# Row sums of adaLN joined with the router in pieces, an early first half of an expert, and the mixers' products spread out

## The chip, the core and the metric

The program runs on one core of one Trainium2 chip. The metric is the time of one execution in device microseconds (us). Times of single instructions come from one profiled execution; the median of the runs is given beside it. TensorE has a matmul side (PE) and a weight-load side (PEld); VectorE is DVE, ScalarE is ACT, GpSimd is POOL and SyncE, which issues most DMAs, is SP. PSUM has eight banks of 128 x 512 floats.

## The reference

Two blocks in a row on 256 tokens of width 1024. Only the parts around the change are shown.

```python
def first_block(x, ...):
    ...
    x = x + merged @ w_o[l]
    h2 = rmsnorm(x, g_ffn[l]).reshape(B * S, D)
    moe = hier_moe(h2, w_rg[l], b_rg[l], w_re[l], b_re[l], w_up[l], w_down[l])
    return x + moe.reshape(B, S, D)

def hier_moe(h, ...):            # 4 groups of 8 experts
    g_logits = h @ w_rg + b_rg   # top-1 group
    e_logits = h @ w_re + b_re   # top-2 experts inside the group
    ...                          # weights of the chosen experts: combine
    for n in range(N_EXPERTS):
        a, b = jnp.split(h @ w_up[n], 2, axis=-1)
        out = out + combine[:, n:n + 1] * ((jax.nn.silu(a) * b) @ w_down[n])

def second_block(x, c, ...):     # two layers
    mod = c_act @ w_ada[l] + b_ada[l]           # nine vectors of adaLN
    h = h + 0.5 * (1.0 + gt1) * swiglu(hn, ...)
    proj = hn @ w_mix_in[l]
    # window attention | RWKV-7 recurrence | short convolution (3 taps)
    mixed = jnp.concatenate([y_att, y_rwkv, y_conv], axis=-1) @ w_mix_out[l]
    h = h + (1.0 + gt2) * mixed
    h = h + 0.5 * (1.0 + gt3) * swiglu(hn, ...)
```

The recurrence of RWKV-7 subtracts `S kk` and adds `v k` to a state S at each token. In the kernel it is worked out in chunks of 64 tokens, so that a triangular matrix of each chunk has to be inverted.

## The kernel before

**Products and banks.** Every engine runs its own instruction list, written out by hand in `build`; the order in it is the order of the work, and semaphores join the engines. On PE, `product(consumer)` hands out banks 0 to 6 in a ring of seven: the n-th product waits until the (n-7)-th has been read by ACT or DVE. `keep_warm(n)` multiplies a matrix of ones with a constant n times, 256 columns each; nobody reads the result. An f32 matmul stands in the trace as two rows, one of type fp32r as one row.

**Start.** PE transposes x (`to_features`), sums squares (`norm_sum`), turns the rows of gains into columns (`to_columns(5)`), and then projects with slabs of `w_in`, 1 MB each, which SP streams into six slots.

**Router and experts.** After the projection `w_o`, DVE norms h in eight chunks and makes the low part `h_lo` of each at once (`norm(..., split=True)`). PE waits for all eight, does the router's 16 matmuls (36 columns each), turns h into tokens (`to_tokens`, into `htok`, f32), and DVE finds each token's group. DVE then signals `ids_ready`, on which SP starts to load experts in the order of the groups; it builds the gathering matrices `perm` and the weights `cin`. `moe` gathers the tokens of the other three groups in eight chunks of 384 columns, `htok` times `perm` in f32, from banks 2 to 7; ACT writes the high part `hg_hi`, DVE the low part. Then come the experts: group 0 in full (eight units of two steps s of 128 tokens), the others in 24 units of one step ("few"). An up matmul is three fp32r ones of 512 columns (high x high, high x low, low x high); `up_high` on ACT and `up_low` on DVE split each slab, `w_hi` has three places. Meanwhile DVE does the row sums of adaLN (`ada_piece`, 1.2 us each).

**Mixers, one in each layer.** After a projection split in parts comes the RWKV chain. `short` are six blocks of eight matmuls for the short convolution's inputs. Four coupling products (AT, BT, C1T, C2T) of eight 64-row matmuls each are masked on DVE. Six levels double the size of the inverted blocks: `off*Tm` on PE, a copy on ACT, `TT*M1` and `M1*TT` on PE, subtractions on DVE; each level also takes a step of window attention, and levels 0 to 3 one `short` block. Then four chunks update the state, the convolution is done on DVE, y is centred and normed, and the output projection runs: four of its eight blocks begin early with the six inputs that are ready (`OUT_EARLY`), `residual` on DVE adds the blocks to x. Before that, DVE splits three slabs of the next dense part (`up_low`); the third one can be loaded only when the first slab of `w_mix_out` is released.

## Time and profile before

| | us |
|---|---|
| median of 3 runs | 1969.59 |
| lowest, highest | 1968.55, 1969.59 |
| the profiled execution | 1968.42 |
| its span, first to last instruction | 1966.6 |
| PE, PEld busy | 1898.4, 1696.2 |
| DVE, ACT busy | 1135.5, 756.5 |

1.8 us of the profiled execution lie outside its span. A row of a timeline gives the start and the length in us, the engine, the line, the output and inputs, and how many instructions are merged; in square brackets, the idle time before it and who ended it. The granted clock (PEclk) of a stretch is a share of 2.4 GHz, so 0.50 is 1.2 GHz. A matmul that writes constants only (`bank<-const`) is a `keep_warm`.

### The profile page before, as it was taken

Reading aid. Unit: us, or ns where it says so; the run is one execution under the profiler, and the core shown is the slowest. Engines: PE = TensorE matmul, PEld = TensorE weight load, DVE = VectorE, ACT = ScalarE, POOL = GpSimd, SP = SyncE. Lnnn points to the kernel's source line nnn. Section 1 sums busy time; section 2 is a strip of 40 time slices with the busy share of each in tenths; the row PEclk is TensorE's granted clock in tenths of the full one; section 3 lists DMA queues with packets and bytes.
Section 4 is the critical chain, followed back from the end, with each engine's and each line's share of the span. In section 5 each row is a group of like instructions: output and inputs, shape, how many; then the busy total and the mean of one; then the engine's idle time right before and its main releaser. Section 6 shows DMA issues by size and latency. Waiting matters only on the chain.

```text
span 1966.6 us, 29769 instructions
## 1 busy us (share of the span) xinstructions
PE 1898.4 (97%) x12380; PEld 1696.2 (86%) x12380; DVE 1135.5 (58%) x1754; ACT 756.5 (38%) x1071; POOL 31.1 (2%) x63
## 2 busy tenths in 40 slices
PE   7999989999999999999999999999999999999998
PEld 6788868778876666999988879999999988879998
DVE  1394043366666655877646548776877547545543
ACT  3222231243444445434443324444444443324442
POOL 6000000000000000000000000000000000000000
PEclk9999999899999999999999999999999999999999
DMA  8244421256699988677541036787676541033441
GB/s 258 92 149 146 145 70 43 108 223 236 253 376 393 366 323 340 243 307 307 193 151 44 22 159 223 307 318 289 240 306 264 165 150 44 23 123 128 180 191 65
DMA packets 124566, 391.56 MB, mean 199 GB/s; under 512 B 11802, under 2 KB 72516, under 8 KB 95120
## 3 DMA queue, kind: packets, MB, share of 16 engines
q1 hardware_dynamic: 122192, 387.71, 52.8%
q8 instruction: 98, 1.61, 0.3%
q0 software_dynamic: 1936, 0.89, 0.2%
q10 hardware_dynamic: 304, 1.06, 0.1%
q14 instruction: 36, 0.29, 0.0%
HBM read 388.58 MB, written 1.05 MB: 198 GB/s over the span
## 4 chain that ended last, share of the span: by engine, by line
PE 87%; DVE 6%; issue 2%; ACT 2%; DMA 2%; SPq 0%; DVEq 0%; ACTq 0%
PE bank L534 86%; DMA slab<-in_w_up 2%; PE bank L569 1%; ACT w_hi L1403 1%; DVE slab_low L1837 0%; DVE hT L1799 0%; DVE tiny L1882 0%; DVE region L2382 0%; ACT L1290 0%; DVE hT L1822 0%; DVE region L1881 0%; ACT rsB L1326 0%; DVE region L2364 0%; DVE region L1901 0%; ACT region L1312 0%
## 5 line engine op out<-in xcount | busy, mean ns | idle before, releaser
L1837 DVE TENSOR_TENSOR slab_low<-slab,w_hi 128x2048 fp32r<-128x2048 f32 x152 | 348.0, 2291 | 216.2 <-ACT w_hi L1403 215.8
L534 PE MATMUL bank<-h_hi,w_hi 128*128 128x256 f32 x1408 | 395.3, 281 | 1.5 <-DVE h_lo L1829 1.5
L534 PE MATMUL bank<-h_lo,w_hi 128*128 128x256 f32 x1408 | 394.7, 280 | 0.0
L534 PE MATMUL bank<-h_hi,slab_low 128*128 128x256 f32 x1408 | 393.3, 279 | 0.0
L1403 ACT ACTIVATE w_hi<-slab 128x2048 fp32r<-128x2048 f32 x152 | 290.7, 1915 | 168.8 <-DMA slab<-in_w_ffn_in 81.9
L534 PEld LDWEIGHTS bank<-h_hi,w_hi 128*128 128x128 f32 x1408 | 264.3, 188 | 3.0 <-issue 3.0
L534 PEld LDWEIGHTS bank<-h_hi,slab_low 128*128 128x128 f32 x1408 | 265.8, 189 | 0.0
L534 PEld LDWEIGHTS bank<-h_lo,w_hi 128*128 128x128 f32 x1408 | 264.9, 188 | 0.0
L534 PE MATMUL bank<-gT_hi,d_hi 128*128 128x256 f32 x832 | 233.7, 281 | 0.8 <-DVE gT_lo L2024 0.8
L534 PE MATMUL bank<-gT_hi,d_low 128*128 128x256 f32 x832 | 233.6, 281 | 0.0
L534 PE MATMUL bank<-gT_lo,d_hi 128*128 128x256 f32 x832 | 233.6, 281 | 0.0
L534 PE MATMUL bank<-hT,slab 128*128 128x256 f32 x960 | 214.2, 383 | 2.1 <-DVE hT L1799 1.8
L534 PEld LDWEIGHTS bank<-hT,slab 128*128 128x128 f32 x960 | 183.2, 192 | 28.9 <-issue 4.1
L1437 ACT ACTIVATE lnt<-bank 128x256 f32<-128x256 f32 x128 | 48.9, 382 | 361.9 <-PE bank L534 359.7
L534 PE MATMUL bank<-region 128*128 128x128 f32 (+4 forms) x1296 | 168.6, 291 | 13.0 <-DVEq L2406 5.0
L534 PEld LDWEIGHTS bank<-region 128*128 128x128 f32 (+2 forms) x1296 | 148.8, 185 | 29.2 <-DVEq L2406 6.4
L534 PEld LDWEIGHTS bank<-gT_hi,d_hi 128*128 128x128 f32 x832 | 156.7, 188 | 1.3 <-issue 1.0
L534 PEld LDWEIGHTS bank<-gT_lo,d_hi 128*128 128x128 f32 x832 | 156.7, 188 | 0.3
L534 PEld LDWEIGHTS bank<-gT_hi,d_low 128*128 128x128 f32 x832 | 156.7, 188 | 0.0
L534 PE MATMUL bank<-region,slab 128*128 128x256 f32 x640 | 141.8, 380 | 1.6 <-DVEq L2177 1.1
L1312 ACT ACTIVATE region<-bank 128x256 f32<-128x256 f32 (+1 forms) x121 | 53.3, 452 | 221.9 <-PE bank L534 221.5
L534 PEld LDWEIGHTS bank<-region,slab 128*128 128x128 f32 x640 | 120.7, 190 | 20.7 <-issue 2.3
(295 smaller groups left out, 2640.6 us busy)
## 6 DMA issues: line engine op xcount, KB each, us to landing
slab<-in_w_ffn_in SPq DMA_DIRECT2D x88, 1024.0 KB, 8.5
slab<-in_w_up SPq DMA_DIRECT2D x64, 1024.0 KB, 9.2
region<-in_w_ada SPq DMA_DIRECT2D x112, 512.0 KB, 6.6
region<-in_w_ffn_out SPq DMA_DIRECT2D x44, 1024.0 KB, 5.0
region<-in_w_down SPq DMA_DIRECT2D x32, 1024.0 KB, 5.6
slab<-in_w_in SPq DMA_DIRECT2D x23, 1024.0 KB, 5.1
slab<-in_w_mix_in SPq DMA_DIRECT2D x20, 1024.0 KB, 8.9
hT<-in_w_ada SPq DMA_DIRECT2D x32, 512.0 KB, 6.0
```

Of the source, the lines that this page charges most:

```text
L534: return nc.tensor.matmul(o, lhsT, rhs, start=start, stop=True, skip_group_check=True)
L569: return nc.tensor.transpose(o, in_, C("eye")[0:k, 0:k])
L1312: read(nc.scalar.activation(dst, src, func, **kw))
L1403: nc.scalar.activation(w_hi[h % 3][:, :], slab[slot][:, :], ACT.Copy).then_inc(S["uhi_ready"], 1)
L1437: nc.scalar.activation(act_s, place(s)[:, 0:T], ACT.Silu).then_inc(S["silu_ready"], 1)
L1837: V_.tensor_tensor(slab_low[slot][:, :], slab[slot][:, :], w_hi[h % 3][:, :].bitcast(F), ALU.subtract)\
```

## The change

- `keep_warm` uses the first 256 columns of the constants (identity and ones), which arrive before the others, instead of `cos`. It is added at the start (4 before x, 3 before the sum of squares, 4 before the columns of gains), and 6 before the index logits; 10 before the router become 4.
- `norm` before the router no longer makes `h_lo`; `router_low` does so in three pieces between DVE's router steps. The router's matmuls run over the chunks of h outside and over tokens inside, with a matmul of constants of 128 columns between chunks.
- The tokens are gathered from two fp32r parts, `htok_hi` and `htok_lo`, each turned from `h_hi` and `h_lo`, with `perm` in fp32r. High and low land in two banks, so there are three places; ACT and DVE each copy one.
- `moe` on PE begins with the first half (four chunks, both steps) of expert 0, before the gather; the second half follows it. ACT and DVE split slabs 0 and 1 before `moe`, ACT with its copies of `htok_lo` and `permT` around them.
- Mixers: level 0 is formed directly (`TT` = identity minus the level-0 part of AT; `Tm` is its transpose). Only AT is coupled first; BT, C1T, C2T follow in levels 1 to 3. `short` blocks move: 0 before the low-rank products, 1 as before, 2 before the levels, 3 in level 1, 4 and 5 in halves of 128 tokens at the start of the four chunks. The convolution is done per 128 channels, the first after chunk 2. The sums of y go to bank 7, with the first early output blocks around them. Five places lose a `keep_warm` (4, 2, 2, 5, 3), one gains 3.

The core of the diff:

```diff
             def moe():
-                quiet()
                 members = [u for u in UNITS if u.seg == 0]
+                slabs_of(members[0])
+                keep_warm(5)
+                for s in range(2):
+                    ring_free(s)
+                for kc in range(KD // 2):
+                    for s in range(2):
+                        m = up_mm(members[0], s, s, kc)
+                m.then_inc(S["half_mid"], 1)
                 pe.wait_ge(S["tok_ready"], w("tok_ready"))
                 for kc in range(KD):
                     gather(kc)
-                pe.wait_ge(S["h_split"], w("h_split", KD))
-                for unit, t, s, pending in SLOTS_OF[0][:-1]:
+                quiet()
+                for s in range(2):
+                    for kc in range(KD // 2, KD):
+                        m = up_mm(members[0], s, s, kc)
+                    m.then_inc(S["up_done"], 1)
+                turn_step(0)
+                for unit, t, s, pending in SLOTS_OF[0][2:-1]:
...
             norm_sum()
-            keep_warm(10)
-
-            for i in range(KD):
+            keep_warm(4)
+
+            idle, ps = product(None), product("dve")
+            for kc in range(KD):
                 pe.wait_ge(S["hn"], w("hn"))
-            ps = product("dve")
-            for t in range(NT):
-                for kc in range(KD):
+                for t in range(NT):
                     m = mm(ps[:, t * 64:t * 64 + 36], hT[:, kc, t * P:(t + 1) * P], router[:, kc, :],
                            t == 0 and kc == 0)
+                if kc < KD - 1:
+                    mm(idle[:, 0:P], C("ones"), const[:, 0:P], True)
             m.then_inc(S["for_dve"], 1)
...
-                    keep_warm(4)
+                    short = projection(hT, 4, "act")
+                    short(0)
                     pe.wait_ge(S["lora_in"], w("lora_in"))
...
-                    for lev in range(6):
+                    short(SHORT_FIRST)
+                    for g in range(2):
+                        pe.wait_ge(S["tt_ready"], w("tt_ready"))
+                        ps = product("act")
+                        for x in range(4):
+                            m = transpose(ps[:, x * P:(x + 1) * P], V["TT"][:, g, x * P:(x + 1) * P])
+                        m.then_inc(S["for_act"], 1)
+                    pe.wait_ge(S["kdup_ready"], w("kdup_ready"))
+                    scores(0)
+                    for lev in range(1, 6):
...
-                        if lev:
-                            output(lev - 1)
-                        if SHORT_FIRST + lev < 6:
-                            short(SHORT_FIRST + lev)
+                        if lev in COUPLED:
+                            coupling(*COUPLED[lev][1:3])
+                        output(lev - 1)
+                        if lev == 1:
+                            short(SHORT_FIRST + 1)
...
                     for c4 in range(T // CHUNK):
                         t, r0 = c4 // 2, (c4 % 2) * CHUNK
+                        short_half(4 + c4 // 2, c4 % 2)
...
-                        keep_warm(2)
+                        if c4 > 1:
+                            keep_warm(2)
...
-                    keep_warm(5)
+                    pe.wait_ge(S["swa_ready"], w("swa_ready"))
+                    pe.wait_ge(S["conv_ready"], w("conv_ready"))
...
+                    out_early(0)
                     pe.wait_ge(S["y_ready"], w("y_ready"))
-                    pair_sum(V["W"], consumer="dve")
-                    keep_warm(3)
+                    mm(bank[7][:, :], C("half"), V["W"], True).then_inc(S["y_mean"], 1)
+                    out_early(1)
                     pe.wait_ge(S["yc_sq"], w("yc_sq"))
                     pair_sum(sq[:, 0:2, :])
...
+                    for b in range(2, OUT_EARLY):
+                        out_early(b)
```

**Where the order moves, PE, router to first expert.** `rscratch,const` is the count of groups, `const,hT` and `const,h_hi` the turning into tokens, `region,sq` the gather. Before:

```order
L534 MATMUL bank<-const 128x256 x10
L534 MATMUL bank<-router,hT 128x36 x16
L569 MATMUL bank<-const,hT 128x128 x8
L534 MATMUL bank<-rscratch,const 128x4 x5
L569 MATMUL bank<-const,hT 128x128 x8
L534 MATMUL bank<-const 128x256 x6
L569 MATMUL bank<-const,region 128x128 x6
L534 MATMUL bank<-const 128x256 x2
L534 MATMUL bank<-rscratch,region 128x8 x6
L534 MATMUL bank<-region,sq 128x384 x16
L534 MATMUL bank<-w_hi_59,h_hi 128x512
```

And after, from the router's last pair:

```order
L538 MATMUL bank<-router,hT 128x36 x2
L579 MATMUL bank<-const,h_hi 128x128 x8
L538 MATMUL bank<-rscratch,const 128x4 x5
L579 MATMUL bank<-const,h_hi 128x128 x8
L538 MATMUL bank<-const 128x256 x4
L579 MATMUL bank<-const,h_lo 128x128 x16
L579 MATMUL bank<-const,perm_r 128x128 x6
L538 MATMUL bank<-const 128x256 x4
L538 MATMUL bank<-rscratch,perm_r 128x8 x6
L538 MATMUL bank<-const 128x256 x5
L538 MATMUL bank<-w_hi_59,h_hi 128x512
```

Sixteen transposes are new, and 24 matmuls of expert 0 now stand where 16 of the gather stood; the gather's 32 come behind them.

**PE, a mixer's coupling and first levels.** `region 128x128` are couplings and levels, `const,region` turned probabilities, `hT,slab` a `short` block. Before:

```order
L534 MATMUL bank<-region,const 128x512
L569 MATMUL bank<-const,region 128x128 x12
L534 MATMUL bank<-region 128x128 x32
L534 MATMUL bank<-region,const 128x256 x2
L534 MATMUL bank<-region 128x128 x26
L534 MATMUL bank<-hT,slab 128x256 x8
L534 MATMUL bank<-region 128x128 x10
L569 MATMUL bank<-const,region 128x128 x2
L534 MATMUL bank<-region 128x128 x16
L534 MATMUL bank<-region 64x128 x2
L534 MATMUL bank<-hT,slab 128x256 x8
```

And after, to the end of level 1:

```order
L538 MATMUL bank<-region,const 128x512
L538 MATMUL bank<-region 128x128 x8
L579 MATMUL bank<-const,region 128x128 x12
L538 MATMUL bank<-region,const 128x256 x2
L538 MATMUL bank<-hT,slab 128x256 x8
L579 MATMUL bank<-const,region 128x128 x8
L538 MATMUL bank<-region 128x128 x12
L579 MATMUL bank<-const,region 128x128 x2
L538 MATMUL bank<-region 128x128 x24
L538 MATMUL bank<-region 64x128 x2
L538 MATMUL bank<-hT,slab 128x256 x8
```

24 of the 32 coupling matmuls left the front for levels 1 to 3, and eight transposes stand where level 0's 24 matmuls stood.

**PE, the end of a mixer.** `region,slab` is the output projection, `region,const 128x512` the sums of y, `sq,const` those of its squares. Before:

```order
L534 MATMUL bank<-region 64x128 x8
L534 MATMUL bank<-const 128x256 x5
L534 MATMUL bank<-region,const 128x512
L534 MATMUL bank<-const 128x256 x3
L534 MATMUL bank<-sq,const 128x512
L534 MATMUL bank<-region,slab 128x256 x64
```

And after:

```order
L538 MATMUL bank<-region 64x128 x8
L538 MATMUL bank<-region,slab 128x256 x6
L538 MATMUL bank<-region,const 128x512
L538 MATMUL bank<-region,slab 128x256 x6
L538 MATMUL bank<-sq,const 128x512
L538 MATMUL bank<-region,slab 128x256 x52
```

Twelve matmuls of the projection took the place of the constants. The squares' product, which takes a bank of the ring, now stands behind the second block of the projection instead of before the first; the sums of y left the ring.

## Rows read from the trace of the kernel before

**Rows 1.** The page: busy time of each engine; the chain, shares by engine.
```profile
PE 1898.4 (97%) x12380; PEld 1696.2 (86%) x12380; DVE 1135.5 (58%) x1754; ACT 756.5 (38%) x1071; POOL 31.1 (2%) x63
...
PE 87%; DVE 6%; issue 2%; ACT 2%; DMA 2%; SPq 0%; DVEq 0%; ACTq 0%
```

**Rows 2.** Timeline, start: start us, length us, engine, line, instructions merged.
```profile
11.79 5.76 PE L534 MATMUL bank<-sq,const 128*128 128x256 f32 x16 [1.60 <-ACT sq L1331]
...
18.91 3.26 DVE L1799 SCALAR_TENSOR_TENSOR hT<-xT,par,rsB 128x256 f32<-128x256 f32 x8
```

**Rows 3.** Timeline from the norm before the router to the gather.
```profile
361.08 1.67 DVE L1799 SCALAR_TENSOR_TENSOR hT<-xT,par,rsB 128x256 f32<-128x256 f32 x4 [3.99 <-ACT rsB L1326]
...
365.94 5.57 PE L534 MATMUL bank<-router,hT 128*128 128x36 f32 x32 [1.53 <-DVE hT L1799]
...
371.62 0.23 DVE L2204 TENSOR_TENSOR rscratch<-bank,bbc 128x72 f32<-128x72 f32 x1 [4.46 <-PE bank L534]
...
375.81 0.16 DVE L2225 COPY tiny<-bank 128x4 f32<-128x4 f32 x1 [1.93 <-PE bank L534]
...
379.62 2.14 SPq L2488 DMA_DIRECT2D slab<-in_w_up  x4
...
386.08 10.56 PE L534 MATMUL bank<-region,sq 128*128 128x384 f32 x32 [0.40 <-issue]
```

**Rows 4.** Windows: length, busy (count) of five engines, PEclk, DMA share, GB/s.
```profile
368.00:370.00 2.00, 2.00 (x11) 2.00 (x11) 0.00 (x0) 0.00 (x0) 0.00 (x0) 0.50 0.00 0
...
402.00:404.00 2.00, 2.00 (x6) 1.52 (x6) 1.51 (x1) 0.00 (x0) 0.00 (x0) 0.50 0.99 410
```

**Rows 5.** The page's costliest groups: splitting a slab, on DVE and on ACT.
```profile
L1837 DVE TENSOR_TENSOR slab_low<-slab,w_hi 128x2048 fp32r<-128x2048 f32 x152 | 348.0, 2291 | 216.2 <-ACT w_hi L1403 215.8
...
L1403 ACT ACTIVATE w_hi<-slab 128x2048 fp32r<-128x2048 f32 x152 | 290.7, 1915 | 168.8 <-DMA slab<-in_w_ffn_in 81.9
```

**Rows 6.** Timeline: the start of step s = 3 (expert 1, second step) on PE.
```profile
419.82 0.51 PE L534 MATMUL bank<-w_hi,h_hi 128*128 128x512 f32 x1 [1.51 <-DVE gT_lo L1970]
```

**Rows 7.** The chain of waits: 24 up matmuls of 512 columns, in the steady run.
```profile
434.52 5.50 PE bank L534 x24
```

**Rows 8.** Timeline, mixer of the first layer: couplings, levels, first chunk.
```profile
1040.21 5.04 PE L534 MATMUL bank<-region 64*128 64x128 f32 x64
...
1041.47 0.69 DVE L2364 TENSOR_TENSOR region<-bank,const 128x512 f32<-128x512 f32 x1 [1.01 <-PE bank L534]
...
1057.23 2.59 PE L534 MATMUL bank<-region 128*128 128x128 f32 x20
...
1078.42 2.59 PE L534 MATMUL bank<-region 128*128 128x128 f32 x20
...
1081.04 0.42 DVE L1881 SCALAR_TENSOR_TENSOR region<-bank,const 128x256 f32<-128x256 f32 x1 [3.36 <-PE bank L534]
...
1089.01 3.00 PE L534 MATMUL bank<-region 128*128 128x128 f32 x20
...
1105.01 2.66 PE L534 MATMUL bank<-region 128*128 128x64 f32 x16 [0.49 <-DVEq L2389]
```

**Rows 9.** Timeline: the starts of the second and third chunk on PE.
```profile
1113.74 3.77 PE L534 MATMUL bank<-region 128*128 128x64 f32 x16 [1.22 <-DVEq L2406]
...
1125.69 1.60 PE L534 MATMUL bank<-region 128*128 128x64 f32 x12
```

**Rows 10.** Windows, columns as in rows 4: two microseconds of the second chunk.
```profile
1116.00:1118.00 2.00, 2.00 (x7) 1.24 (x6) 0.46 (x1) 0.00 (x0) 0.00 (x0) 0.50 0.00 0
```

**Rows 11.** Timeline, end of the mixer: output projection, third slab, residual.
```profile
1145.77 27.79 PE L534 MATMUL bank<-region,slab 128*128 128x256 f32 x128
...
1164.66 1.91 ACT L1403 ACTIVATE w_hi<-slab 128x2048 fp32r<-128x2048 f32 x1 [10.87 <-DMA slab<-in_w_ffn_in]
...
1168.82 4.27 DVE L2185 SCALAR_TENSOR_TENSOR xT<-bank,modg,xT 128x256 f32<-128x256 f32 x7
```

More of the change, by code:

```diff
@@ L124 @@
     "ulo_ready": "the low part of half of a unit's up weights", "dlo_ready": "that of its down weights",
-    "gt_lo": "a step's turned activations, low part", "hg_split": "both parts of a chunk of the gathered h",
+    "gt_lo": "a step's turned activations, low part", "hg_low": "a chunk of the gathered h, low part",
     "h_split": "both parts of a chunk of the normalised residual",
@@ L1070, in _ @@
             m.then_inc(S["for_dve"], 1)
-            to_tokens(1)
-            keep_warm(6)
+            to_tokens(h_hi, 1)
+            keep_warm(4)
+            pe.wait_ge(S["h_split"], w("h_split", KD))
+            for t in range(NT):
+                to_tokens(h_lo, t)
             pe.wait_ge(S["perm_ready"], w("perm_ready"))
@@ L1125, in _ @@
                     pair_sum(sq[:, 6, :])
-                    short = projection(hT, 6, "act")
-                    for b in range(SHORT_FIRST):
+                    for b in range(1, SHORT_FIRST):
                         short(b)
@@ L1677, in _ @@
                 tables(SIG)
+                short = [V[dst][:, c, :] for dst in ("cb", "cc", "ch") for c in range(2)]
                 act.wait_ge(S["pm_ready"], w("pm_ready"))
@@ L1815, in norm, with router_low @@
                                          ALU.subtract).then_inc(S["h_split"], 1)
+            def router_low(first, end):
+                for j in range(first, end):
+                    dve.wait_ge(S["h_high"], w("h_high"))
+                    V_.tensor_tensor(h_lo[:, j, :], hT[:, j, :], h_hi[:, j, :].bitcast(F), ALU.subtract)\
+                        .then_inc(S["h_split"], 1)
             def norm_dense(gain, shift):
@@ L2196, in _ @@
             link(V_.memset(clist, PAD))
+            norm(xT, lambda j: col("g_ffn", j), hT)
+            router_low(0, 1)
             def wide(v, n):
```

203 lines of the change are left out of this document (121 added, 82 removed).

## The prediction

> **What bounds the kernel now.** The page's first part and its chain come first: PE is busy 97% of the span and holds 87% of the chain [rows 1]. So only what shortens or slows PE's list counts, and it can shorten in three ways: matmuls that nobody reads go, a wait goes, or the same matmul runs at 2.4 instead of 1.2 GHz. Next come the timeline of PE at the places of the change, for its waits, and the windows there, for the clock. Both PEclk windows near the router and the one in a chunk show 0.50 [rows 4, 10].
>
> Prices for one matmul: 5.50/24 = 0.229 us for 512 columns [rows 7], so 0.172 for 384; 27.79/128 = 0.217 for a row of 256 f32 columns [rows 11], so a `keep_warm` matmul (two rows) costs 0.43 and a `short` block (16 rows) 3.47; a coupling product is 5.04/4 = 1.26 [rows 8]. The sum is made against the profiled execution, 1968.42.
>
> **Start: -1.2.** The first `norm_sum` takes 5.76 for 16 rows [rows 2] where 16 x 0.217 = 3.47 is the quick price: 2.3 to gain if constants before it bring the quick pace. The four constants before `to_columns` cost about 1.0 (partly beside ACT's squares). DVE's norm, which starts at 18.91 [rows 2], then starts at about 17.7. Bounds: -2.5 (those four are covered) and +1.0 (the pace doesn't come). I take the middle, since the matmuls just ahead are what differs from the quick places. The six before the index logits (2.6) I put at nothing: they stand where PE waits for DVE anyway; uncovered they cost 2.6.
>
> **Router to experts: -3.1.**
> - DVE's four last norm steps start at 361.08 with a step of 1.67/4 = 0.42, and the router's 5.57 begin at 365.94, after all eight [rows 3]. In pieces, the first matmuls start with the first chunk; 32 rows of 0.118 (36 columns, clock now full) and seven constants of 128 columns (14 rows, 0.115) are 5.4 us. With the first chunks at about 361.8 PE ends at 367.2 and DVE adds the bias at 367.4 instead of 371.62: -4.2. The count of groups likewise, 375.81 to 371.7: -4.1, as `router_low(1, 6)` (some 2.0) lies beside the transposing of `h_hi`. Uncovered it would add up to 2.
> - SP's first w_up moves from 379.62 [rows 3] to about 375.5. 1.5 MB (weights and slab 0) at 410 GB/s [rows 4] are 3.8, with 1.2 of latency (estimate): slab 0 is there at 380.5. ACT then does `up_high(0)` (1.92 [rows 5]) to 382.4, four copies of `htok_lo` (512 columns; estimate 2.1) to 384.5, `up_high(1)` to 386.4, and only then `permT`, to 387.0. The second step's bank is the one that this copy frees, so PE starts its first up matmul at about 387.1, after an idle stretch near 381.
> - Then 24 ups 5.5 [rows 7], to 392.6; gather 32 x 0.172 = 5.5 instead of 10.56 [rows 3], to 398.1; second half 5.5, to 403.6. Then the steps of turning, each behind `hidden` or DVE's `up_low` (2.29 [rows 5]) and a piece of adaLN: about 1.1, 2.7 and 2.0 of idle, and the rest of the first unit. Step s=3 starts at 415.6 instead of 419.82 [rows 6]: -4.2.
> - The idle stretch before expert 0 may drop the clock, as it stands at 0.50 at 402:404 [rows 4] behind today's wait for slab_low: +1.1. Net -3.1. Behind it the experts keep the shift, since PE or the loads set their pace as before. Bounds: -8 (no wait before the first half) and 0 (all given back to the waits for slabs).
>
> **Mixers: -10.8 each, -21.6 in all.** Stamps are of the first layer's mixer [rows 8].
> - The chain up to the couplings stays (the moved `short(0)` takes 3.47 where four constants took 1.7; the second gain, a warmer clock, gives it back). DVE's first AT mask stands at 1041.47, after 1.01 of idle; with AT alone in front it stands at 1040.5.
> - Of DVE's masks of four couplings and the subtractions of level 0, eight steps of about 0.69 remain before level 1, with small gaps: 5.8, so its inputs are ready at 1046.3 and PE starts level 1 at 1046.4 instead of 1057.23: -10.8. What PE drops is 24 coupling matmuls (3 x 1.26, moved) and level 0's products.
> - Level 1 has to wait for its probabilities: DVE's scaled comes 2.6 after a level's start (1081.04 - 1078.42), then ACT's exponentials; estimate +1.9. It also holds a coupling (1.26) and `short(3)` (3.47). Level 2 starts at 1060.5, 14.1 later.
> - Levels 2 and 3 lose the `short` (3.47) and gain a coupling (1.26). Today a level is (1078.42 - 1057.23)/2 = 10.6, 1089.01 - 1078.42 = 10.6; PE's list alone is then 10.6 - 3.47 + 1.26 = 8.4, and DVE's chain (scaled at +2.6, two subtractions with their products 4.4, the couple's two masks 1.4, probabilities 0.9, less overlap) gives 8.8. I take 8.8: level 3 at 1069.3, level 4 at 1078.2, against 1089.01.
> - Levels 4 and 5 had no `short`: 1105.01 - 1089.01 = 16.0 stays, chunk 0 at 1094.2: -10.8.
> - Chunks: two `short` blocks (in four halves of 1.74, 7.0) come in. Against that go the idle stretches (0.49 and 1.22 [rows 8, 9], and more inside a chunk), two `keep_warm(2)` (1.7), and the half clock of chunk 1 (0.50 at 1116:1118 [rows 10]; chunk 1 takes 1125.69 - 1113.74 = 11.95 [rows 9], full pace would save some 2 to 3). Net +1.0.
> - The end: the constants (5 + 3, 3.4) become output matmuls, and the convolution leaves a third of its time behind the last chunk. The projection's first matmul comes at about 1140.0 instead of 1145.77 [rows 11] on the old stamps, its early blocks end 4.0 sooner. But of its blocks p0 to p7, p6 now takes the bank of p0, since the squares' product sits between p1 and p2; before, p6 took the bank of that product, read long ago. p0 is read by DVE's residual, which starts at 1168.82 only, behind `up_low` of the third slab, for which ACT waits 10.87 on its DMA and starts at 1164.66 [rows 11]. That load is released by the projection, so it comes 4.0 sooner: ACT 1160.7, DVE's residual at 1164.9, first bank free at 1165.4. PE is at p6 at 1162.4: 3.0 of stall. So only 1.0 of the 4.0 stays.
> - Sum: -10.8 + 1.0 - 1.0 = -10.8. Bounds -17 (no stall, chunk 1 wins 3 more) and -4 (DVE sets levels 1 to 3, stall full).
>
> **Sum.** -1.2 - 3.1 - 21.6 = -25.9: 1942.5 for the profiled execution. The median of the runs lies 1969.59 - 1968.42 = 1.17 above it: 1943.7, I say 1943.5.
>
> **The rivals.**
> - *The third slab comes early enough.* Were it loaded before p6's turn, the 3.0 of stall fall away in both mixers: -6, 1937.5. For it: SP has fewer waits ahead once the blocks start earlier. Against: ACT's 10.87 of idle there is all DMA [rows 11]. 0.12.
> - *DVE becomes the engine of the levels.* A level's DVE work grows by two masks (1.4); if they lie on the loop from scaled to scaled, a cycle is 10 + 1.4 = 11.4 instead of 8.8: +2.6 for levels 2 and 3 and two mixers, +10, 1953.5. For it: DVE and PE already alternate there (3.36 of idle before scaled [rows 8]). Against: the same 3.36 is room enough for 1.4. 0.20.
> - *Transposes lower the clock.* Behind the 16 of `h_lo` the first half of expert 0 would run at 1.2 GHz like the row at 402:404 [rows 4]: 5.5 becomes up to 11, less what it waits for slabs anyway, some +2; level 0 gives +1 in each mixer. +4, 1947.5. The transposes by themselves are 24 of thousands. 0.07. The Trainium skill, "TensorE: Matmul & The Clock Gate", § Part 4: PE-mode transpose, speaks for it: a matmul in transpose mode doesn't bring the full clock on, since it isn't counted as a busy PE in the same way. By that rule the sum would be -22, by the row alone -26; no run so far shows which.
> - *Slower: the levels lose their cover.* Levels 2 and 3 lose the solid 16 rows of `short`, and levels hang on DVE between small products. If the granted clock falls to 0.50 in levels 2 to 5, each one of PE's 6 us of matmuls doubles: +6 in each of 4 levels and two mixers, +48: 1991. It decides from the fifth of the eight levels on (5 x 6 = 30 > 25.9). Against: levels 4 and 5 of today have no `short` and still run their first 20 rows in 3.00 [rows 8], 0.150 a row beside 2.59/20 = 0.130 in level 3. 0.05.
> - *The change doesn't do what it says*: fewer constants leave the router at 0.50 as today [rows 4] (+2), inside the forecast's range.
>
> **Chances.** 0.56 for the forecast, whose own bounds from the parts are about 1936 to 1951; then as above. The range 1932 to 1954 takes in the early slab and DVE's levels. A measurement can tell about 0.2%, 4 us, from no change, here 1965.7 to 1973.5. Faster 0.92 (all but the last rival, and a small remainder where several losses meet), same 0.03, slower 0.05.
>
> **What would show it.** In the profile after: DVE's bias add some 4 us earlier; PEclk 1.00 while the router runs; the first up matmul waits on ACT's copy, at about 387, and s=3 starts near 415.6 (all less the start's 1.2); level starts of PE 14, 8.8 and 8.8 apart, with PE, not DVE, idle for the shorter time; the chunks one by one within 1 us of before; a gap of 3 us in front of the seventh block of the output projection, ended by DVE's residual, with ACT waiting for the third slab's DMA. It would be wrong if levels 2 and 3 take over 10, if PEclk shows 0.50 in a level, or if the steps after expert 0's second half wait for slabs more than 6 us in all.

## The result and the profile of the changed kernel

The changed kernel takes 1944.7 us (median of 4 runs, 1941.4 to 1949.9), the kernel before, beside it, 1969.1. The ratio is 0.9885 with a 95% interval of 0.9861 to 0.9909: faster. The profiled execution took 1947.8, its span is 1946.0. So the forecast of 1943.5 came out for the median. For the profiled execution it was 1942.5, and that one is 5.3 longer. The stages of the two profiles tell how much of this was right.

Both kernels do `norm_sum` (`bank<-sq,const`, 16 rows) before each large part, and its start divides the span. Stages in us, before and after, as the difference of two such starts:

| stage | before | after | moved | forecast |
|---|---|---|---|---|
| start, to 36.93 | 36.93 | 35.95 | -1.0 | -1.2 |
| attention and projections, to 356.48 | 319.55 | 316.47 | -3.1 | 0 |
| router and experts, to 776.15 | 419.67 | 419.69 | 0.0 | -3.1 |
| first dense part, to 969.68 | 193.53 | 193.53 | 0.0 | 0 |
| first mixer, to 1173.40 | 203.72 | 194.99 | -8.7 | -10.8 |
| two dense parts and second mixer, to 1763.73 | 590.33 | 581.02 | -9.3 | -10.8 |
| the last dense part and the end | 202.87 | 204.35 | +1.5 | 0 |

The page of the changed kernel, the engines and the chain, to be held against [rows 1]: PE has 17.3 us less to do and is as much the bound as before.

```profile
PE 1881.1 (97%) x12374; PEld 1684.9 (87%) x12374; DVE 1131.8 (58%) x1746; ACT 759.9 (39%) x1079; POOL 31.1 (2%) x63
...
PE 86%; DVE 6%; ACT 3%; issue 2%; DMA 2%; SPq 0%; DVEq 0%; ACTq 0%
```

The timeline of the start (start us, length us, then as in [rows 2]). `norm_sum` takes 3.72 instead of 5.76, and DVE's norm starts at 17.93 instead of 18.91, 0.2 from the forecast of 17.7. Between them stand 1.89 us of constants, which nothing covers.

```profile
11.77 3.72 PE L538 MATMUL bank<-sq,const 128*128 128x256 f32 x16 [0.83 <-ACT sq L1400]
15.33 1.89 PE L538 MATMUL bank<-const 128*128 128x256 f32 x8
...
17.93 3.26 DVE L1873 SCALAR_TENSOR_TENSOR hT<-xT,par,rsB 128x256 f32<-128x256 f32 x8
```

The timeline from the router to the experts, in order of time, against [rows 3, 6]. Everything here stands 4.06 earlier already before the router (352.42 against 356.48).

```profile
363.08 0.23 DVE L2282 TENSOR_TENSOR rscratch<-bank,bbc 128x72 f32<-128x72 f32 x1 [2.13 <-PE bank L538]
...
377.51 1.91 ACT L1472 ACTIVATE w_hi<-slab 128x2048 fp32r<-128x2048 f32 x1 [2.98 <-DMA slab<-in_w_up]
379.33 2.04 ACT L1381 ACTIVATE htok_lo<-bank 128x512 fp32r<-128x512 f32 x4
...
380.05 1.83 PE L538 MATMUL bank<-rscratch,perm_r 128*128 128x8 f32 x12 [4.46 <-ACT htok_lo L1381]
381.73 4.62 PE L538 MATMUL bank<-const 128*128 128x256 f32 x10
...
383.30 0.85 ACT L1381 ACTIVATE region<-bank 128x512 f32<-128x512 f32 x2
...
385.78 0.99 PE L538 MATMUL bank<-w_hi,h_hi 128*128 128x512 f32 x1
...
414.94 0.47 PE L538 MATMUL bank<-w_hi,h_hi 128*128 128x512 f32 x1 [1.64 <-DVE gT_lo L2051]
```

And a window there (length, busy and count of five engines, PEclk, DMA share, GB/s):

```profile
384.00:386.00 2.00, 2.00 (x7) 1.64 (x5) 1.79 (x1) 1.43 (x2) 0.00 (x0) 0.50 0.97 410
```

DVE's bias add is 8.5 earlier than 371.62, so 4.5 of its own. By s=3 only 4.88 - 4.06 = 0.8 are left. In between PE waits 4.46 for ACT's copies of `htok_lo`, and the five constants behind that wait run at 1.2 GHz: 4.62 instead of 2.2. ACT's copies of `permT`, on which the first up matmul was thought to wait, are done at 384.15 (383.30 + 0.85), but PE comes to it only at 385.78.

The timeline of the first mixer, against [rows 8, 9]. `bank<-hT,slab` is a short block, DVE's rows are the start of `scaled` in levels 2 and 3 and that of the next one, the `128x128` block is the half at the start of chunk 0.

```profile
1042.63 3.33 PE L538 MATMUL bank<-region 64*128 64x128 f32 x24
...
1057.11 2.59 PE L538 MATMUL bank<-region 128*128 128x128 f32 x20
...
1059.73 0.42 DVE L1962 SCALAR_TENSOR_TENSOR region<-bank,const 128x256 f32<-128x256 f32 x1 [3.62 <-PE bank L538]
...
1068.57 0.42 DVE L1962 SCALAR_TENSOR_TENSOR region<-bank,const 128x256 f32<-128x256 f32 x1
...
1077.84 0.69 DVE L1962 SCALAR_TENSOR_TENSOR region<-bank,const 128x512 f32<-128x512 f32 x1 [0.60 <-PE bank L538]
...
1090.24 2.05 PE L538 MATMUL bank<-hT,slab 128*128 128x128 f32 x16
...
1124.89 4.52 PE L538 MATMUL bank<-region,slab 128*128 128x256 f32 x12 [1.36 <-issue]
```

Level 1 starts near 1042.7, level 2 at 1057.1 (14.4 later), then `scaled` follows itself by 8.84 and 9.27. Chunk 0 begins at 1090.24. With the 4.04 by which the mixer starts earlier, 1105.01 becomes 1100.97, so the front of the mixer gave 10.7: forecast 10.8.

The end of both mixers, against [rows 11]: PE's early and late blocks, ACT's split of the third slab, DVE's residual, and PE's resumption, in the first layer and in the second.

```profile
1133.55 15.70 PE L538 MATMUL bank<-region,slab 128*128 128x256 f32 x72
...
1147.18 1.91 ACT L1472 ACTIVATE w_hi<-slab 128x2048 fp32r<-128x2048 f32 x1 [5.61 <-DMA slab<-in_w_ffn_in]
...
1151.33 3.63 DVE L2264 SCALAR_TENSOR_TENSOR xT<-bank,modg,xT 128x256 f32<-128x256 f32 x6
...
1151.96 8.83 PE L538 MATMUL bank<-region,slab 128*128 128x256 f32 x32 [2.71 <-DVE xT L2264]
...
1733.27 8.54 PE L538 MATMUL bank<-region,slab 128*128 128x256 f32 x32 [2.78 <-DVE xT L2264]
```

That is the stall that was forecast, with the engine that was named: 2.71 and 2.78 of it, 3.0 said. But the 32 rows behind it (p6 and p7) take 8.83 and 8.54, where 32 x 0.217 is 6.9, and the first early blocks take 4.52 for 12 rows, where 2.6 is the quick price. The windows say why:

```profile
1126.00:1128.00 2.00, 2.00 (x6) 1.56 (x5) 0.00 (x0) 0.00 (x0) 0.00 (x0) 0.50 0.00 0
...
1152.00:1154.00 2.00, 2.00 (x6) 1.64 (x7) 1.56 (x4) 0.83 (x2) 0.00 (x0) 0.61 1.03 424
```

### The profile page after: what moved, and what is told of

Same layout as the page of the kernel before. It is cut to its first block, busy times and chain, and to the rows that moved or that the text cites. A ratio compares the mean times of both kernels' runs of the same rounds, so it can differ in the third digit from the quotient of the medians.

```text
span 1946.0 us, 29754 instructions
## 1 busy us (share of the span) xinstructions
PE 1881.1 (97%) x12374; PEld 1684.9 (87%) x12374; DVE 1131.8 (58%) x1746; ACT 759.9 (39%) x1079; POOL 31.1 (2%) x63
## 3 DMA queue, kind: packets, MB, share of 16 engines
HBM read 388.58 MB, written 1.05 MB: 200 GB/s over the span
## 4 chain that ended last, share of the span: by engine, by line
PE 86%; DVE 6%; ACT 3%; issue 2%; DMA 2%; SPq 0%; DVEq 0%; ACTq 0%
PE bank L538 85%; DMA slab<-in_w_up 2%; PE bank L579 1%; ACT w_hi L1472 1%; DVE slab_low L1918 1%; DMA slab<-in_w_ffn_in 0%; DVE region L1931 0%; ACT rsB L1395 0%; DVE region L1982 0%; DVE tiny L1963 0%; DVE region L2470 0%; DVE region L2447 0%; DVE region L2468 0%; DVE hT L1903 0%; DVE region L1962 0%
## 5 line engine op out<-in xcount | busy, mean ns | idle before, releaser
L538 PE MATMUL bank<-hT,slab 128*128 128x256 f32 (+1 forms) x1024 | 215.2, 370 | 1.7 <-DVE hT L1873 1.2
L538 PE MATMUL bank<-region 128*128 128x128 f32 (+5 forms) x1200 | 154.7, 288 | 6.7 <-DVEq L2435 2.4
L538 PE MATMUL bank<-region,slab 128*128 128x256 f32 x640 | 147.9, 390 | 9.8 <-DVE xT L2264 5.5
L538 PEld LDWEIGHTS bank<-region 128*128 128x128 f32 (+2 forms) x1200 | 135.0, 181 | 22.1 <-issue 4.6
L2008 DVE SCALAR_TENSOR_TENSOR region<-region 128x1024 f32<-128x1024 f32 x112 | 136.4, 1220 | 1.6 <-DMA region<-in_w_ada 1.6
```

What stands on the lines that cost most here:

```text
L538: return nc.tensor.matmul(o, lhsT, rhs, start=start, stop=True, skip_group_check=True)
L2008: V_.scalar_tensor_tensor(part, part, 1.0, c_act, ALU.mult, ALU.mult, accum_out=ada[:, o:o + 1])\
```

## The experiments

**The theory** going in: the gain is the front of the mixers, and each mixer gives some of it back in a stall of the ring, whose price is more than its idle time. **The rival**: the gain comes as well from the new router and from a clock that happened to be full at 50 and 290 us. First the two halves of the change by themselves. The median of the kernel before, timed beside the first four variants, was 1964.9 (17 runs, 1959.1 to 1978.7).

**The mixers alone.** The kernel before with, for the mixers only, everything that the change does:

```diff
-                    for lev in range(6):
+                    for lev in range(1, 6):
...
+                        if lev in COUPLED:
+                            coupling(*COUPLED[lev][1:3])
...
+                        short_half(4 + c4 // 2, c4 % 2)
...
+                    out_early(0)
```

> The kernel before with the mixers' part of the change alone (level 0 formed directly, the couplings and short blocks spread, the new end). In the profile of the changed kernel each mixer moved by 8.7 and 9.3 us (from the squares' sum before it to the one behind it, 1026 and 1173 before). If the parts add, this kernel gains 18 us: about 1951, and its other stages stay within 2 us of before. Rival: part of what the mixers gain is only a clock that was full by chance in one profile; then this kernel shows half clock at other places in the mixers and gains 12 or less. The end stall before the seventh output block (2.7 us, ended by DVE's residual) should be there in both mixers.

Measured: 1945.7 us, 19.3 below the kernel before (18 expected), ratio 0.9885 (0.9859 to 0.9911), as the whole change had. In the profile the first mixer is 10.1 shorter than before, the part to 1740.70 behind it 10.5: forecast 10.8 each. The stall is there in both (first and second layer), somewhat longer. But in the second the clock is 1.00 behind it (1734:1736), and the same 32 rows take 7.14 instead of 8.83:

```profile
1152.23 8.83 PE L536 MATMUL bank<-region,slab 128*128 128x256 f32 x32 [3.04 <-DVE xT L2220]
...
1733.72 7.14 PE L536 MATMUL bank<-region,slab 128*128 128x256 f32 x32 [3.01 <-DVE xT L2220]
```

The rest of the profile is not as before everywhere, though: the experts' stage took 417.5 instead of 419.7 with unchanged code. About 2 us of one profile's stage there are not the change's.

**The start, the router and the experts alone.**

```diff
+            keep_warm(4)
             to_features(xin, "x_in")
+            keep_warm(3)
             norm_sum()
+            keep_warm(4)
...
+            up_high(0)
             for t in range(NT):
                 for x in range(2):
-                    evac(htok[:, t, x * 512:(x + 1) * 512], 512)
+                    evac(htok_lo[:, t, x * 512:(x + 1) * 512], 512)
```

> The kernel before with the start, the router and the experts' part alone, the mixers as before. Theory: start -1.0 (adaLN's first slabs arrive on time either way), router to step s=3 of the experts -0.8 only, since the first half of expert 0 waits for constants at half clock and runs half its matmuls at half clock; the rest, about 3 us between 46 and 292 us, was the clock of stretches that the change doesn't touch. Then this kernel gains 2 to 5 us: about 1965. Rival: the stretches at 46:52 and 288:292 run at full clock because of the new start; then they are at full clock here too and it gains 5 to 7, about 1963.

Measured: 1961.8 us, ratio 0.9992 (0.9965 to 1.0019): by time, no difference that these runs can tell, 3.1 us between the medians. In the profile the start gave 1.05; the stage to the router took 319.57, as before, with PEclk 0.50 at 50:52 and 0.64 at 290:292. So the new start alone doesn't always bring the full clock there. Whether it makes it likelier stays open: of the eleven profiles of this case that have the constants in front of the first sum, or transposes in their place, eight show the full clock near 290 and three, this one among them, the half; the three without either (the kernel before, the mixers alone, and the start without constants) show the half. From the router's `norm_sum` to the third turning of activations (`bank<-const,lnt`, in step s=3) it was 66.2 before, 63.1 here: -3.1, the term of the sum. The changed kernel's own profile shows 65.3 for the same code: its clock stayed at 0.50 up to near 388. Over all eight profiles that have this code here unchanged (the changed kernel, this one and six below) it is 62.1 to 65.7, so that -3.1 is one draw between -0.6 and -4.1. The rival is half right: 3 us of the changed profile's 20.6 are the clock of a stretch that the change doesn't touch, but they don't carry the gain.

**The squares' bank, taken earlier.**

```diff
+                    sq_bank = product("act")
                     out_early(0)
...
-                    pair_sum(sq[:, 0:2, :])
+                    mm(sq_bank[:, :], C("half"), sq[:, 0:2, :], True).then_inc(S["for_act"], 1)
```

> The changed kernel, with one edit at the end of a mixer: the bank for the squares' product is taken before the first early output block instead of between the second and the third, so that the seventh block (p6) takes a bank that was read long ago. Theory of the prediction (the stall is the price of the ring's order): the wait of 2.7 us before p6 goes, and the half clock behind it (1152 to 1156) with it; p7 then waits for the bank of p0, up to 1 us: -2 to -4 per mixer, 4 to 8 in all, about 1939. Rival: the wait only moves to p7 and to the next dense part, whose first units need DVE's low parts and norm anyway: -1 or less in all.

Measured: 1934.1 us, ratio 0.9829 (0.9803 to 0.9855), faster than both kernels, and by more than I expected. The projection runs in one piece:

```profile
1126.86 22.61 PE L538 MATMUL bank<-region,slab 128*128 128x256 f32 x104
...
1140.58 1.91 ACT L1473 ACTIVATE w_hi<-slab 128x2048 fp32r<-128x2048 f32 x1 [5.69 <-DMA slab<-in_w_ffn_in]
...
1144.73 4.26 DVE L2265 SCALAR_TENSOR_TENSOR xT<-bank,modg,xT 128x256 f32<-128x256 f32 x7
```

The third slab and DVE's residual come as late, relative to PE, as with the stall (14.6 and 18.7 behind the squares' sum, 14.5 and 18.6 with it). Only the bank is another. From the squares' sum to the next `norm_sum` it is 1149.31 - 1126.01 = 23.3; in the changed kernel 27.9 and 27.7, with the mixers alone 28.3 and, in the second layer, 26.6. The stall's whole price is thus 4.4 to 5.0 where the clock falls behind it, and 3.2 in the one mixer where it doesn't: 2.7 to 3.0 of idle time, and a clock at 0.50 that costs most of the rest. The remaining part of the 6.3 that the first mixer gained over the changed kernel is the other half-clock stretch (1126:1128), absent here although PE's rows and waits before it are the same (0.66 and 1.36 of idle). It isn't the bank's doing alone: two later profiles with the bank edit have it in their first mixer (4.24 and 4.48 for these 12 rows instead of 2.83), while the second mixer of the changed kernel and both with the mixers alone lack it. Why it falls in some and not in others stays open.

Nor does the edit rule the stall out. In one of the 18 mixers profiled with it, the first of the start without constants below, the third slab is split 17.3 behind the squares' sum instead of 14.6, and PE waits in front of the last block:

```profile
1145.72 1.91 ACT L1471 ACTIVATE w_hi<-slab 128x2048 fp32r<-128x2048 f32 x1 [8.38 <-DMA slab<-in_w_ffn_in]
...
1150.40 5.41 PE L538 MATMUL bank<-region,slab 128*128 128x256 f32 x16 [1.93 <-DVE xT L2263]
```

**Filling the wait before the experts.**

```diff
-            keep_warm(4)
+            keep_warm(14)
             pe.wait_ge(S["cin_ready"], w("cin_ready"))
```

> The changed kernel with 14 instead of 4 constants matmuls before the product of the weights (L1116's keep_warm(4)), which fill the 4.46 us in which PE waits for ACT's copy of htok_lo. Theory: the half clock at 381 to 387 comes from that idle stretch; with it filled the granted clock stays at 1.00, the five constants behind take 2.2 instead of 4.6, and the first half of expert 0 starts 1.6 earlier and ends 2.5 earlier; step s=3 starts 1 to 2.5 earlier. Rival: ACT and DVE with the next slabs set the first units, so step s=3 stays within 0.5 us of 414.9 and only the clock figures change.

Measured: 1941.1 us, ratio 0.9859 (0.983 to 0.9887).

```profile
371.75 6.21 PE L538 MATMUL bank<-const 128*128 128x256 f32 x28
...
381.74 0.47 PE L538 MATMUL bank<-w_hi,h_hi 128*128 128x512 f32 x1 [0.19 <-ACT region L1381]
```

The clock stays at 1.00 (382:384), and the first up matmul now does wait on the copy of `permT`, as the prediction had said for the changed kernel. From the router's sum to the third turning it is 62.2, against 65.3 in the changed kernel's profile and 63.5 in that of the bank edit. These pairs give 1.3 to 3.1. But the code without the filling took 62.1 in its shortest profile, so that the gain lies in not losing the clock near 381, and isn't shown beyond that. The two mixers stall as in the changed kernel: 28.0 and 28.1 from the squares' sum to the next `norm_sum`. By time the intervals of the two kernels overlap (0.9830 to 0.9887, 0.9861 to 0.9909).

**Both edits.**

```diff
-            keep_warm(4)
+            keep_warm(14)
             pe.wait_ge(S["cin_ready"], w("cin_ready"))
...
+                    sq_bank = product("act")
                     out_early(0)
```

> The changed kernel with both edits: the squares' bank taken before the early output blocks, and 14 constants before the product of the weights. If the two gains add (11 and some 3 us against the changed kernel's own median) it stands 3 us below the kernel with the bank edit alone, about 1931, with one half-clock stretch fewer near 381. Rival: the half clock only moves to another place (the wait near 404), then it is within 1 us of the kernel with the bank edit alone.

Measured: 1928.0 us (1927.4 to 1930.7), ratio 0.981 (0.9788 to 0.9832); the kernel before, beside this and the next three variants, had 1965.4. This is the best version that was timed more than once, 1.9% below the kernel before where the change alone was 1.15%. That it beats the bank edit alone (0.9803 to 0.9855) is likely, not shown: the intervals overlap. The third turning comes 62.6 behind the router's sum, the mixers are as with the bank edit alone (188.7 for the first). While PE works, the profile has PEclk below 0.97 in two stretches only, near 366 and near 407.

**All couplings in front again.**

```diff
                     coupling("be", "al")
+                    for lev in COUPLED:
+                        coupling(*COUPLED[lev][1:3])
...
-                        if lev in COUPLED:
-                            coupling(*COUPLED[lev][1:3])
```

and the same for `couple` on DVE.

> The kernel with the bank edit, but all four coupling products and their masks in front of the levels again, as in the kernel before; the rest of the change stays. Theory: in levels 1 to 3 DVE is busy without a gap (cycle 8.84 us, of which the two masks are 1.45), so spreading the masks only moves them. Here level 1 starts 6 x 0.72 = 4.3 us later and levels 1 to 3 are 1.4 shorter each: +0 to +1.5 per mixer, the level cycle 7.4. Rival (that of the change's design): masks are free inside the levels; then the cycle stays above 8.5 and each mixer is 4 us longer.

Measured: 1947.9 us, ratio 0.9903 (0.9876 to 0.993). This expectation was wrong: the mixers are 9.2 and 6.5 longer than with the bank edit alone, not 0 to 1.5. DVE's six masks, PE's products of level 1, and the turnings of levels 2 and 3:

```profile
1041.99 4.32 DVE L2448 TENSOR_TENSOR region<-bank,const 128x512 f32<-128x512 f32 x6
```

```profile
1050.60 3.33 PE L538 MATMUL bank<-region 64*128 64x128 f32 x24
...
1067.65 0.44 PE L579 MATMUL bank<-const,region 128*128 128x128 f32 x2
...
1075.81 0.44 PE L579 MATMUL bank<-const,region 128*128 128x128 f32 x2
```

The levels shrink by less than the two masks: 8.16 between turnings instead of 8.90, since PE now waits 0.74 for DVE in between. And the front grows by more than the masks: level 1 starts 28.46 behind the sum of squares (1050.60 - 1022.14), with the masks spread 19.57 (1037.64 - 1018.07). Of these 8.9 the masks are 4.3; PE also waits 1.98 and 2.01 for banks that DVE's masks free, its clock is at 0.50 from 1038 to 1046, and `short(2)` comes behind all that. So the spread was worth 6.5 to 9.2 in a mixer, half-clock stretches of both mixers' fronts included. Forming level 0 directly, the other half of the front's gain, was not tried by itself.

**Short blocks 4 and 5 whole, in levels 2 and 3.**

```diff
-                        if lev == 1:
-                            short(SHORT_FIRST + 1)
+                        if lev < 4:
+                            short(SHORT_FIRST + lev)
...
-                        short_half(4 + c4 // 2, c4 % 2)
```

> The kernel with the bank edit, but short blocks 4 and 5 whole in levels 2 and 3 as before, not in halves in the chunks. Theory: levels 2 and 3 grow from 8.8 to about 12 (PE's list 8.6 + 3.47), the four chunks lose four halves of 1.9 but get idle stretches back, so they shrink by 5.5 at full clock: +1 per mixer; and if the clock falls in the chunks as in the kernel before (0.50 at 1114 to 1120), +4. Rival: the levels take the blocks for nothing beside DVE's chain; then each mixer is 5 us shorter.

Measured: 1957.6 us, ratio 0.9949 (0.9929 to 0.9969), each mixer 10.7 longer than with the bank edit. Levels 2 and 3 grew by 3.35 and 3.45, as expected. The four chunks, from chunk 0 to the first output matmul, did not shrink at all: 38.0 without the halves, 34.65 with them.

```profile
1097.46 2.66 PE L538 MATMUL bank<-region 128*128 128x64 f32 x16 [0.49 <-DVEq L2474]
...
1105.39 3.21 PE L538 MATMUL bank<-region 128*128 128x64 f32 x16 [1.22 <-DVEq L2504]
...
1135.47 2.83 PE L538 MATMUL bank<-region,slab 128*128 128x256 f32 x12 [1.36 <-issue]
```

```profile
1110.00:1112.00 2.00, 2.00 (x10) 1.91 (x9) 0.68 (x5) 1.37 (x6) 0.00 (x0) 0.50 0.03 8
```

The idle times of [rows 8, 9], 0.49 and 1.22, are back, and the clock is at 0.50 from 1108 to 1124. The halves don't only fill waits. With them the chunks ran at 2.4 GHz, in both mixers, and that is worth more than the work that they bring. Whether constants in their places would do the same was not tried.

**The gather before the first half of expert 0.**

```diff
-                keep_warm(5)
+                pe.wait_ge(S["tok_ready"], w("tok_ready"))
+                for kc in range(KD):
+                    gather(kc)
                 for s in range(2):
                     ring_free(s)
```

> The kernel with the bank edit, but with the gather first and then the first half of expert 0, and without the five constants ahead of it. The gather needs only htok_lo (copied 4 us before the copies of permT on which the first half waits), so it can run where PE now runs constants. Theory: the early first half hides nothing that the gather would not hide; the gather starts near 381.5, the second half ends about 2 us earlier, step s=3 and all after it 0 to 2 us earlier. Rival: the early first half is worth the slabs' latency; then the copies of ACT, now behind up_high(1) and permT, hold the gather and everything comes 2 us or more later.

Measured: 1932.1 us, ratio 0.9828 (0.9803 to 0.9853), within 2 us of the bank edit, and the third turning 64.0 behind the router's sum instead of 63.5.

```profile
381.63 0.98 PE L538 MATMUL bank<-perm_r,htok_hi 128*128 128x384 f32 x2 [1.55 <-ACT region L1381]
```

The gather waits for the same copy of `permT` as the first half does, because one of its banks is the one that this copy reads. So neither theory: the order of gather and first half makes no difference that the runs can tell (the 0.5 is less than the clock moves this stretch from profile to profile), as both stand behind the same copy.

**The start**, one execution each, all with the bank edit: 1936.9 us without the constants, 1932.8 with transposes, 1927.9 without the four before the columns, where the kernel before took 1968.1. Their stages are read, not these times. Without the constants before x and before the first sum:

```diff
-            keep_warm(4)
             to_features(xin, "x_in")
-            keep_warm(3)
             norm_sum()
```

> The kernel with the bank edit, without the constants before x and before the first sum of squares. Theory: the pace of the first norm_sum comes from what PE did just before; without constants it is as before, 16 rows in about 5.8 us (0.36 a row) instead of 3.7, and DVE's first norm comes 1 us later or not at all later, as the columns of gains wait for rows.

With transposes in their place:

```diff
-            keep_warm(4)
+            idle = product(None)
+            for _ in range(16):
+                transpose(idle[:, 0:P], C("eye"))
             to_features(xin, "x_in")
-            keep_warm(3)
+            idle = product(None)
+            for _ in range(12):
+                transpose(idle[:, 0:P], C("eye"))
```

> The kernel with the bank edit, with transposes of the identity (16 before x, 12 before the first sum of squares) in place of the constants there, about the same busy time. If transposes keep the pace as products do, the first norm_sum takes 3.7 us for 16 rows and x's transposes run at the pace of the changed kernel (16 in 3.1). If the Trainium skill's rule on transpose mode (TensorE: Matmul & The Clock Gate, Part 4: PE-mode transpose) holds here, norm_sum takes 5.8 as without any.

Without the constants, then with the transposes (x's 16 transposes, then the sum):

```profile
11.99 5.22 PE L538 MATMUL bank<-sq,const 128*128 128x256 f32 x16 [1.60 <-ACT sq L1399]
```

```profile
6.43 2.37 PE L579 MATMUL bank<-const,region 128*128 128x128 f32 x16
...
11.65 3.72 PE L538 MATMUL bank<-sq,const 128*128 128x256 f32 x16 [1.54 <-ACT sq L1405]
```

5.22 without (5.8 expected), 3.72 with transposes, 3.72 with products. Transposes keep the pace as products do. Without either DVE's norm started at 19.65, 1.7 later than with the bank edit alone.

Without the four constants before the columns of gains:

```diff
             norm_sum()
-            keep_warm(4)
             pe.wait_ge(S["rows_in"], 16 * sum(1 for _ in first_rows()))
```

> The kernel with the bank edit, without the four constants before the columns of gains. These run from 15.33 to 17.2 and the columns come right behind them, then ACT's copy and DVE's norm at 17.93. Theory: without them the columns come at 15.5 and DVE's norm starts when ACT's rsB is there, about 1 us earlier, 16.9. Rival: the rows or rsB are late anyway, and DVE's norm stays within 0.2 of 17.9.

```profile
14.75 0.23 PE L579 MATMUL bank<-const,silu 16*128 16x16 f32 x1
...
16.18 3.26 DVE L1873 SCALAR_TENSOR_TENSOR hT<-xT,par,rsB 128x256 f32<-128x256 f32 x8
```

DVE's norm starts at 16.18 instead of 17.98, and the second sum of squares at 34.20 instead of 36.00: -1.8, where I expected 1. The sum itself started 0.7 earlier there (11.10), so about 1.1 are the constants'.

**Without the constants between the router's pairs.**

```diff
-                if kc < KD - 1:
-                    mm(idle[:, 0:P], C("ones"), const[:, 0:P], True)
```

> The kernel with the bank edit, without the seven 128-column products of constants between the router's pairs. With them PE works through the router without an idle stretch at full clock and then shows 0.50 at 366 to 371. Theory: DVE paces the router's pairs (0.67 us each), so the router ends at the same time within 0.3, with gaps in it, and the clock falls at the latest where it falls now; the constants buy nothing measurable. Rival: the router's last pair and the bias come 1 us or more later, since its rows then run at half clock.

```profile
356.03 4.08 PE L538 MATMUL bank<-router,hT 128*128 128x36 f32 x32
```

```profile
360.15 0.23 DVE L2281 TENSOR_TENSOR rscratch<-bank,bbc 128x72 f32<-128x72 f32 x1 [0.92 <-PE bank L538]
```

One execution, 1929.6 us. Counted from the router's `norm_sum` (350.70 here, 352.45 with the bank edit) the bias add comes at 9.45 instead of 10.66: the constants cost 1.2 at this place, since PE, not DVE, paced the pairs with them (0.67 a pair, DVE's norm 0.41). Without them the clock is at 0.50 from 360 to 369, and the third turning comes at 63.2 instead of 63.5. What is saved at the router is lost behind it in this profile. That the constants buy nothing is borne out so far; but the router did not end within 0.3, and the reason given, that DVE sets the pace, was wrong.

## Why the prediction was right

The total was right and so were most of its terms, but for the profiled execution the sum was 5.3 too low. Part of the agreement is luck: the experts came out 3.1, the mixers 2.1 and 1.5 and the end 1.5 behind the forecast, and a stretch that the forecast held unchanged gave 3.1 back. Point by point:

- **Start** (-1.2, measured -1.0 in both kernels with it). Its 1.0 for the constants before the columns was right too: about 1.1.
- **Router to experts** (-3.1; measured -3.1 alone, -2.7 with the bank edit, -0.9 in the changed kernel's profile). The bias add was right within 0.3. Behind it two steps were off. The slab was split 1.1 later than said, on equal stamps: 6.8 behind its issue (370.73), where 3.8 and a latency of 1.2, which no row gave, had been added up. And the constants in `moe` were taken to be covered at full clock, while the idle stretch that the prediction itself named brought the half clock on before them, not behind: PE came to its first up matmul 2.7 later than said, and ran part of the first half at half clock. That is 3.4 of the 4.2 in the changed profile. Where the clock came back sooner, 3.1 or 2.7 were left, so that the right number owes something to the 1.1 which the sum had set aside for the clock, and to the profile that is taken. The router itself ran at PEclk 1.00, as said; the 0.50 came behind it, near 368.
- **Experts after that** (keep the shift). In the changed profile 0.9 was lost between 419 and 776, with 0.50 at 624:626; in the other kernels with this code the stage is 2.4 to 6.1 shorter than 419.7. But with the old router it varies by 2.2 as well.
- **Mixers' front** (-10.8; measured -10.7). Level 1 at its place, level 2 14.4 later (14.1 said), 8.84 for the next (8.8 said), 9.27 for the third. The rival in which DVE sets the levels at 11.4 is out: DVE is busy nearly without a gap in levels 2 and 3, and the cycle is 8.84 nevertheless. The masks fill part of what was 3.36 of idle.
- **Chunks** (+1.0 with the early output at -5.8, so -4.8; measured 34.65 against 40.76, -6.1). The half clock of chunk 1 went, as said. What this part did not see is that the halves keep it away.
- **The end** (stall 3.0; measured 2.7 and 2.8 idle, ended by DVE's residual, the third slab waiting on its DMA). This is the term that was mis-sized: the sum counted the idle time alone, and in the changed kernel the stall costs 4.6 and 4.4 with the half clock behind it. With the half clock at the first early blocks (1.7, first mixer) that is why the mixers' stages gave 8.7 and 9.3 instead of 10.8. The rival in which the slab comes early enough is out.
- **Outside the change** (0; measured -3.1 and +1.5). The clock at 50:52 and near 290 was full in the changed profile and half in both kernels with one half of the change; the last dense part is longer by a stretch at 0.50 (1938:1940).
- **The rivals on the clock.** Transposes weren't seen to lower it. In the changed kernel PEclk stays at 1.00 from 372 to 380, behind the 16 of `h_lo` at 370.25, and with the later wait filled the first half of expert 0 ran at 1.00. The rule that speaks for that rival (the Trainium skill, "TensorE: Matmul & The Clock Gate", § Part 4: PE-mode transpose) isn't borne out either at the start, by 3.72 against 5.22 above, though both rows stand at a granted clock of 1.00. The slower side, half clock in the levels, didn't come: no window between 1042 and 1122 is below 0.97. The mechanism is real, though, and one stage further on. Without the halves it takes the chunks, and then 10.7 of each mixer go (6.8 of it in levels 2 and 3, where the blocks then stand, and 3.4 in the chunks).

Taken together, the mixers give 10.1 and 10.5 by themselves against 10.8, and are nearly the whole change: 1945.7 us with them alone, 1944.7 with all. The router's half of the code made about 3 us between the medians, which the runs can't tell from nothing.

## What to carry to other kernels

A ring of banks makes the order of products part of the timing. When a product moves, count for every later one whose bank it now inherits and when that is read. Here taking one bank two blocks earlier was worth 11 us, nearly half as much again as the change; by the profiles some 9 of them are the two stalls, the rest goes with the clock.

Price a stall of PE with the clock behind it: 2.7 to 3.0 us of idle time cost 4.4 to 5.0 in five mixers, and 3.2 in one where the clock held. For the same reason real work moved into a chain of short waits can be worth more than its own length, and constants do more in the wait than behind it: behind it ten rows of them took 4.62 at 1.2 GHz and themselves held up the first real matmul.

## What was not expected of the hardware

- The clock fell or held at the same place in the program, with the same rows and waits before it, from one profile to the next: at the first early blocks of the output projection in 5 of 24 profiled mixers, with and without the bank edit; near 50 and 290 in some profiles and not in others. Each such stretch is 1.4 to 3 us. The same code from the second sum of squares to the router took 314.8 to 319.7 us, and from there to the third turning 62.1 to 65.7. Differences under 5 us between two profiles need a count of such stretches first.
- Transposes of the identity (28 of them) kept TensorE at its quick pace as well as matmuls: `norm_sum` 3.72 with either, 5.22 with neither. x's own 16 transposes then took 2.37 instead of 3.65.
- That slower `norm_sum` at the start (5.76, 5.22) stands where the profile gives the granted clock as 1.00; the slow pace there is not in that row. What makes it slow isn't shown.
